# Output projection and feed-forward as one stage in blocks of 512 tokens, with the residual kept on the chip

## The chip, the cores and the metric

The kernel runs on one core of a Trainium2 chip. The metric is the device time of one execution in microseconds (us); lower is better.

## What is computed

One layer of a hybrid decoder (2048 tokens, model width 1024, FFN width 2816). Three token mixers run in parallel and write their outputs into one matrix of 1024 rows of tokens; the change begins behind them. In the words of the reference:

```python
mix = jnp.concatenate([out_a, out_b, out_c], axis=-1) @ w_out
x = x + gate1 * mix

h = rms_norm(x, norm2_gain) * (1.0 + scale2) + shift2
gt, up = jnp.split(h @ ffn_w_gate_up, 2, axis=-1)
x = x + gate2 * ((jax.nn.silu(gt) * up) @ ffn_w_down)

def rms_norm(x, gain):
    xf = x.astype(jnp.float32)
    y = xf * lax.rsqrt(jnp.mean(xf * xf, axis=-1, keepdims=True) + EPS)
    return (y * gain.astype(jnp.float32)).astype(x.dtype)
```

## The kernel before

Everything is stored transposed: features over the 128 partitions (KD = 8 tiles of 128 for the model width, KF = 22 for the FFN width), tokens along the free axis. Five stages follow one another, each in a block of its own with a barrier over all engines at its end: the input projection with the recurrent mixer (`project_in_and_recur`), the operands of the forgetting attention, that attention, the gated linear attention, the output projection (`project_out`) and the feed-forward (`feed_forward`). Within a stage each engine runs its own list of instructions in order, and waits on semaphores; nothing but these lists and waits sets the order. A stage can't load anything before the barrier ahead of it has opened.

Every product of two float32 matrices is made of three float32r matmuls (`split_products`, L77 to L79): each operand is split into a high part (a copy into float32r) and a low part (the value less its high part). For weights, ScalarE makes the high part and GpSimd the low part, for activations ScalarE and VectorE. One matmul takes a 128x128 tile of weights against 512 tokens.

`project_out` (L1308) loads the eight 128x2048 tiles of `mix_dram` through two buffers (`po_slot`), splits them (L1376 ScalarE, L1404 VectorE), and runs over eight output tiles m; each is 8 x 4 x 3 = 96 matmuls into four banks of 512 tokens. VectorE multiplies by gate1 and adds the residual x (L1409). ScalarE stores the result in HBM (`x_dram`, L1386 and L1391) and squares it (L1388, L1393), GpSimd sums the squares. After the last tile, TensorE takes the mean over the features with a matrix of 1/1024 (L1433, L1436), and ScalarE the root (L1396).

`feed_forward` (L1439) runs over four blocks t of 512 tokens. ScalarE loads the block of x2 back from HBM (L1515, 2 MB); VectorE inverts the root (L1593), scales (L1598), and together with ScalarE makes the split normalised input h (L1511, L1605, L1608). Then come 22 units of gate and up (48 matmuls each; their weights come in one transfer of 1 MB, L1482) and 16 units of down (33 matmuls, 704 KB, L1486; two units for each output tile). Weights have two buffers at every step. The next block's h is made in the down units of the block before. VectorE forms silu(g) * u (L1622) and its low part (L1624), and the output y = x2 + gate2 * d (L1634), for which ScalarE loads x2 from HBM once more (L1535) and stores y (L1539).

The first stage, `project_in_and_recur`, is not touched. It holds 96 units of 24 matmuls (8 x 3) whose weights go through the chain L153 (SP, 512 KB), L239 (ScalarE, high part), L201 (GpSimd, low part) with RAW, HI, LO = 2, 3, 2 buffers, and its instructions are written out, not looped. Its x comes in the same queue, 2 MB for each block (L179).

These lines give the waits of a weight unit there:

```python
                def weights(j):
                    if j >= RAW:
                        sp.wait_ge(lo_ready, j - RAW + 1)
                    sp.dma_start(w_raw[:, j % RAW], w_in[j % N_PROJ]).then_inc(w_sem[j % RAW], 16)
                def low(j):
                    pool.wait_ge(hi_ready, j + 1)
                    if j >= LO:
                        pool.wait_ge(unit_done, j - LO + 1)
```

## Time and profile before

| what | value |
|---|---|
| runs of the kernel before | 3228.06, 3219.3, 3227.46 us (median 3227.46) |
| the profiled execution | 3219.62 us, of which the span of instructions is 3217.8 us |
| TensorE busy in the span | 2821.8 us (88%), mean granted clock 0.926 |
| output projection, first DMA issue to its last product | 1529.85 to about 1726.6 us |
| from there to the first product of the feed-forward | to 1767.27 us |
| feed-forward, first to last product | 1767.27 to about 3214.25 us |

The profile shows one execution; times are from the start of its span. A matmul's printed duration contains the pipeline behind it, so the pitch from one matmul's start to the next is what a matmul costs in a row of many. In a list of waits, the engine named behind the arrow is the one that came last.

### The profile page before, as it was taken

Reading aid. Unit: us, or ns where it says so; the run is one execution under the profiler, and the core shown is the slowest. Engines: PE = TensorE matmul, PEld = TensorE weight load, DVE = VectorE, ACT = ScalarE, POOL = GpSimd, SP = SyncE. Lnnn points to the kernel's source line nnn. Section 1 sums busy time; section 2 is a strip of 40 time slices with the busy share of each in tenths; the row PEclk is TensorE's granted clock in tenths of the full one; section 3 lists DMA queues with packets and bytes.
Section 4 is the critical chain, followed back from the end, with each engine's and each line's share of the span. In section 5 each row is a group of like instructions: output and inputs, shape, how many; then the busy total and the mean of one; then the engine's idle time right before and its main releaser. Section 6 shows DMA issues by size and latency. Waiting matters only on the chain. (4 is left out here: it accounts for less than half of the span.)

```text
span 3217.8 us, 34182 instructions
## 1 busy us (share of the span) xinstructions
PE 2821.8 (88%) x12359; PEld 2250.3 (70%) x12359; DVE 1547.8 (48%) x1627; ACT 1090.5 (34%) x1400; POOL 1088.3 (34%) x420
## 2 busy tenths in 40 slices
PE   3898999945887879556795999999999999999999
PEld 2686878821666667334584888878888788888887
DVE  6878786434565656545214454224440444224420
ACT  2333342341475757443212333222221222222221
POOL 2444454401121212100232343444444443444443
PEclk9999999975798989656898999999999999999999
DMA  5555534436211110200523222442234322432233
GB/s 212 193 173 171 172 125 134 138 131 187 52 47 47 46 47 7 115 0 25 220 108 128 100 92 91 126 147 95 100 98 131 136 91 92 122 125 104 91 98 104
DMA packets 86971, 355.99 MB, mean 111 GB/s; under 512 B 9622, under 2 KB 11430, under 8 KB 64690
## 3 DMA queue, kind: packets, MB, share of 16 engines
q1 hardware_dynamic: 67760, 312.81, 29.1%
q10 hardware_dynamic: 19024, 41.95, 4.3%
q8 instruction: 41, 0.67, 0.1%
q14 instruction: 50, 0.41, 0.0%
q0 software_dynamic: 96, 0.15, 0.0%
HBM read 298.15 MB, written 56.72 MB: 110 GB/s over the span
## 5 line engine op out<-in xcount | busy, mean ns | idle before, releaser
L1492 POOL TENSOR_TENSOR ff_w_lo<-ff_w_raw,ff_w_hi 128x2048 fp32r<-128x2048 f32 (+1 forms) x152 | 613.6, 4037 | 875.9 <-ACT ff_w_hi L1521 875.9
L1624 DVE TENSOR_TENSOR ff_a_lo<-ff_gated,ff_a_hi 128x512 f32 x88 | 382.2, 4343 | 148.4 <-ACT ff_a_hi L1531 148.4
L1521 ACT ACTIVATE ff_w_hi<-ff_w_raw 128x2048 fp32r<-128x2048 f32 (+1 forms) x152 | 256.2, 1686 | 356.0 <-PE ff_d_ps L79 356.0
L201 POOL TENSOR_TENSOR w_lo<-w_raw,w_hi 128x1024 fp32r<-128x1024 f32 x96 | 239.2, 2493 | 286.4 <-PE g_ps L79 220.7
L77 PE MATMUL g_ps<-h_hi,w_hi 128*128 128x512 f32 x768 | 309.4, 403 | 8.5 <-POOL w_lo L201 4.8
L77 PE MATMUL ff_g_ps<-ff_h_hi,ff_w_hi 128*128 128x512 f32 x704 | 275.7, 392 | 37.8 <-DVE ff_h_lo L1608 31.9
L78 PE MATMUL g_ps<-h_lo,w_hi 128*128 128x512 f32 x768 | 301.1, 392 | 0.0
L79 PE MATMUL g_ps<-h_hi,w_lo 128*128 128x512 f32 x768 | 301.1, 392 | 0.0
L79 PE MATMUL ff_g_ps<-ff_h_hi,ff_w_lo 128*128 128x512 f32 x704 | 275.5, 391 | 0.0
L78 PE MATMUL ff_g_ps<-ff_h_lo,ff_w_hi 128*128 128x512 f32 x704 | 275.5, 391 | 0.0
L77 PE MATMUL ff_u_ps<-ff_h_hi,ff_w_hi 128*128 128x512 f32 x704 | 273.9, 389 | 0.0
L78 PE MATMUL ff_u_ps<-ff_h_lo,ff_w_hi 128*128 128x512 f32 x704 | 273.9, 389 | 0.0
L77 PE MATMUL ff_d_ps<-ff_a_hi,ff_w_hi 128*128 128x512 f32 x704 | 273.9, 389 | 0.0
L78 PE MATMUL ff_d_ps<-ff_a_lo,ff_w_hi 128*128 128x512 f32 x704 | 273.9, 389 | 0.0
L79 PE MATMUL ff_d_ps<-ff_a_hi,ff_w_lo 128*128 128x512 f32 x704 | 273.9, 389 | 0.0
L79 PE MATMUL ff_u_ps<-ff_h_hi,ff_w_lo 128*128 128x512 f32 x704 | 273.9, 389 | 0.0
L1527 ACT ACTIVATE ff_silu<-ff_g_ps 128x512 f32<-128x512 f32 x88 | 52.7, 599 | 600.9 <-PE ff_u_ps L79 600.8
L810 POOL TENSOR_TENSOR fa_p_lo<-fa_probs,fa_p_hi 128x512 fp32r<-128x512 f32 (+3 forms) x78 | 93.2, 1195 | 403.4 <-ACT fa_p_hi L847 403.4
L239 ACT ACTIVATE w_hi<-w_raw 128x1024 fp32r<-128x1024 f32 x96 | 101.8, 1060 | 368.4 <-DMA w_raw<-in_w_in 297.4
L874 DVE TENSOR_REDUCE fa_ch_max<-fa_s_ps 128x1 f32<-128x512 f32 (+2 forms) x262 | 158.8, 607 | 138.4 <-PE fa_s_ps L930 77.2
L1622 DVE TENSOR_TENSOR ff_gated<-ff_silu,ff_u_ps 128x512 f32<-128x512 f32 x88 | 60.4, 687 | 341.0 <-ACT ff_silu L1527 341.0
L1634 DVE SCALAR_TENSOR_TENSOR ff_gated<-ff_d_ps,mod,ff_x_res 128x512 f32<-128x512 f32 x32 | 24.0, 751 | 401.9 <-PE ff_d_ps L79 401.9
(249 smaller groups left out, 5455.5 us busy)
## 6 DMA issues: line engine op xcount, KB each, us to landing
ff_w_raw<-in_w_gate_up SPq DMA_DIRECT2D x88, 1024.0 KB, 4.8
w_raw<-in_w_in SPq DMA_DIRECT2D x96, 512.0 KB, 4.0
ff_w_raw<-in_w_down SPq DMA_DIRECT2D x64, 704.0 KB, 4.1
mod_w<-in_w_mod SPq DMA_DIRECT2D x24, 1024.0 KB, 5.5
proj_dram<-stage SPq DMA_DIRECT2D x72, 256.0 KB, 3.2
po_slot<-mix_dram SPq DMA_DIRECT2D x8, 1024.0 KB, 4.9
po_slot<-in_xT SPq DMA_DIRECT2D x8, 1024.0 KB, 4.8
x_dram<-po_slot ACTq DMA_DIRECT2D x8, 1024.0 KB, 3.9
```

Of the source, the lines that this page charges most:

```text
L77: nc.tensor.matmul(out, hi, act_hi, start=first, stop=False)
L78: nc.tensor.matmul(out, hi, act_lo, start=False, stop=False)
L79: return nc.tensor.matmul(out, lo, act_hi, start=False, stop=last)
L201: nc.gpsimd.tensor_tensor(w_lo[:, j % LO], w_raw[:, j % RAW], w_hi[:, j % HI].bitcast(F32), ALU.subtract).then_inc(lo_ready, 1)
L239: nc.scalar.activation(w_hi[:, j % HI], w_raw[:, j % RAW], ACT.Copy).then_inc(hi_ready, 1)
L810: nc.gpsimd.tensor_tensor(p_lo[:, m % PB, r * P:BLK], probs[:, m % PB, r * P:BLK], p_hi[:, m % PB, r * P:BLK].bitcast(F32), ALU.subtract). ...
L874: nc.vector.tensor_reduce(ch_max[:, u % 2, i, c:c + 1], s_ps[:, n % SB, 0:w], AX.X, ALU.max).then_inc(max_done, 1)
L1492: nc.gpsimd.tensor_tensor(w_lo[:, s, size(up)], w_raw[:, s, size(up)], w_hi[:, s, size(up)].bitcast(F32), ALU.subtract).then_inc(lo_ready, 1)
L1521: nc.scalar.activation(w_hi[:, s, size(up)], w_raw[:, s, size(up)], ACT.Copy).then_inc(hi_ready, 1)
L1527: nc.scalar.activation(silu[:, s], g_ps[:, s], ACT.Silu).then_inc(silu_ready, 1)
L1622: nc.vector.tensor_tensor(gated[:, s], silu[:, s], u_ps[:, s], ALU.mult).then_inc(gated_ready, 1)
L1624: nc.vector.tensor_tensor(a_lo[:, bass.ds(n, 1)].rearrange("p o n -> p (o n)"), gated[:, s], a_hi[:, bass.ds(n, 1)].rearrange("p o n -> p ...
```

## The change

`project_out` and `feed_forward` become one stage, `out_and_feed_forward`, with one list of 272 units, each with one load of weights: 8 units "o" (an output tile of the output projection for 512 tokens, 24 matmuls), then for each block 22 pairs "g", "u" (24 matmuls each), four output tiles of down ("d", two units of 33 matmuls each), the eight "o" units of the next block, and the other four output tiles of down. The weights of a gate and up pair come as two transfers of 512 KB. Those of the output projection are loaded and split four times, once for each block. The weight chain has the buffers and waits of the first stage (RAW, HI, LO = 2, 3, 2). x2 stays in SBUF, in two blocks of 512 tokens (`ff_x2`), so that the stores to `x_dram` and the loads from it are gone; x is loaded into it by SP (2 MB for a block, `residual`). The squares are summed by VectorE on 512 tokens; the mean (`mean`) is one matmul for each block. For block 0 it stands behind the eighth "o" unit with the whole norm after it; for later blocks it stands behind the ninth half-tile of down, and the norm is made during the rest. The mixers' outputs for block 0 come in eight transfers of 256 KB, each with a semaphore of its own; the constant for the mean is the last of the first loads, and TensorE waits for it at the mean. The stage's instructions are written out, not looped. All loads and stores are issued by SP.

```diff
...
-def feed_forward(nc, vec, mod, rms_all, w_gate_up, w_down, x2, yT):
...
+def out_and_feed_forward(nc, vec, mod, xT, w_out, w_gate_up, w_down, consts, mix, yT):
...
+    W_MAX = HALF * P
+    units = [("o", 0, m, 0) for m in range(KD)]
+    for b in range(NBLK):
+        for n in range(KF):
+            units += [("g", b, n, 0), ("u", b, n, 0)]
+        units += [("d", b, m, s) for m in range(HALF_KD) for s in range(2)]
+        if b + 1 < NBLK:
+            units += [("o", b + 1, m, 0) for m in range(KD)]
+        units += [("d", b, m, s) for m in range(HALF_KD, KD) for s in range(2)]
+    at = {u: j for j, u in enumerate(units)}
+    N = len(units)
+    width = lambda u: HALF * P if u[0] == "d" else KD * P
+    d_order = {u[:3]: i for i, u in enumerate([u for u in units if u[0] == "o" or (u[0] == "d" and u[3] == 1)])}
+    HI, LO, RAW, DB = 3, 2, 2, 3
...
-        w_hi, w_lo = sb("ff_w_hi", [P, 2, 2 * KD * P], F32R), sb("ff_w_lo", [P, 2, 2 * KD * P], F32R)
+        x2 = sb("ff_x2", [P, 2, KD, BLK])
+        w_raw = sb("ff_w_raw", [P, RAW, W_MAX])
+        w_hi, w_lo = sb("ff_w_hi", [P, HI, W_MAX], F32R), sb("ff_w_lo", [P, LO, W_MAX], F32R)
...
+        g_ps, u_ps, d_ps, n_ps = ps("ff_g_ps", [P, 2, BLK]), ps("ff_u_ps", [P, 2, BLK]), ps("ff_d_ps", [P, DB, BLK]), ps("ff_n_ps", [P, BLK])
...
+                def weights(j):
+                    kind, b, i, s = units[j]
+                    if j >= RAW:
+                        sp.wait_ge(lo_ready, j - RAW + 1)
+                    src = {"o": lambda: w_out[i], "g": lambda: w_gate_up[i, :, 0:KD * P], "u": lambda: w_gate_up[i, :, KD * P:], "d": lambda: w_down[2 * i + s]}[kind]()
+                    sp.dma_start(w_raw[:, j % RAW, 0:width(units[j])], src).then_inc(w_in[j % RAW], 16)
...
+                weights(0)
+                for k in range(KD):
+                    sp.dma_start(x2[:, 1, k], mix[k, :, cols(0)]).then_inc(mix0_in[k], 16)
+                    if k == 1:
+                        weights(1)
+                residual(0)
+                sp.dma_start(mean_ones[:], consts[:, C_MEAN * P:(C_MEAN + 1) * P]).then_inc(const_in, 16)
+                for j in range(N):
+                    kind, b, i, s = units[j]
+                    if j + RAW < N:
+                        weights(j + RAW)
+                    if kind == "g" and i == 2 and b + 1 < NBLK:
+                        residual(b + 1)
+                    if kind == "d" and b + 1 < NBLK and i < HALF_KD:
+                        k = 2 * i + s
+                        if k < 2:
+                            sp.wait_ge(gated_ready, KF * (b + 1))
+                        else:
+                            sp.wait_ge(mix_ready, KD * (b + 1) + k - 1)
+                        sp.dma_start(silu[:, k % 2], mix[k, :, cols(b + 1)]).then_inc(mix_in[k % 2], 16)
...
+                def high(j):
+                    wide = slice(0, width(units[j]))
+                    act.wait_ge(w_in[j % RAW], 16 * (j // RAW + 1))
+                    if j >= HI:
+                        act.wait_ge(unit_done, j - HI + 1)
+                    nc.scalar.activation(w_hi[:, j % HI, wide], w_raw[:, j % RAW, wide], ACT.Copy).then_inc(hi_ready, 1)
+                def mix_high(b, k):
+                    act.wait_ge(*landed(b, k))
+                    if b >= 1:
+                        act.wait_ge(unit_done, at["u", b - 1, KF - 1, 0] + 1)
+                    nc.scalar.activation(h_hi[:, k], staged(b, k), ACT.Copy).then_inc(mix_hi, 1)
...
+                high(0)
+                for k in range(2):
+                    mix_high(0, k)
+                high(1)
+                for k in range(2, KD):
+                    mix_high(0, k)
+                for j in range(N + 1):
+                    if j + 2 < N:
+                        high(j + 2)
+                    if j == 0:
+                        continue
...
+                    if kind == "o" and b == 0 and i == KD - 1:
+                        root(0)
+                        for k in range(KD):
+                            norm_high(0, k)
+                    if kind == "d" and b + 1 < NBLK and i >= HALF_KD:
+                        q = 2 * (i - HALF_KD) + s
+                        if q == 0:
+                            root(b + 1)
+                        for k in pairs_at(q):
+                            norm_high(b + 1, k)
...
+                def scale(b, k):
+                    if k >= 2:
+                        dve.wait_ge(h_ready, KD * b + k - 1)
+                    nc.vector.scalar_tensor_tensor(out=silu[:, k % 2], in0=x2[:, b % 2, k], scalar=scale_a[:, k:k + 1], in1=rstd[:],
+                                                   op0=ALU.mult, op1=ALU.mult).then_inc(xs_ready, 1)
+                def norm_low(b, k):
+                    dve.wait_ge(h_hi_ready, KD * b + k + 1)
+                    nc.vector.scalar_tensor_tensor(out=h_lo[:, k], in0=silu[:, k % 2], scalar=mod[:, SHIFT2 + k:SHIFT2 + k + 1], in1=h_hi[:, k].bitcast(F32),
+                                                   op0=ALU.add, op1=ALU.subtract).then_inc(h_ready, 1)
...
+                        if b == 0 and i == KD - 1:
+                            invert(0)
+                            scale(0, 0)
+                            for k in range(KD):
+                                if k + 1 < KD:
+                                    scale(0, k + 1)
+                                norm_low(0, k)
...
+                def mean(b):
+                    pe.wait_ge(const_in, 16)
+                    pe.wait_ge(summed, (KD - 1) * (b + 1))
+                    if b >= 1:
+                        pe.wait_ge(rms_ready, b)
+                    nc.tensor.matmul(n_ps[:], mean_ones[:], sq_sum[:], start=True, stop=True).then_inc(mean_done, 1)
...
+                        for k in range(KD):
+                            if i == 0:
+                                pe.wait_ge(mix_ready, KD * b + k + 1)
+                            last = split_products(nc, d_ps[:, d % DB], tiles(w_hi, hi, k), tiles(w_lo, lo, k), h_hi[:, k], h_lo[:, k], k == 0, k == KD - 1)
```

The order of three places, as the compiler has it. In these rows the tensor `ff_x2` reads `ff_x`.

SP at the start of the output projection, before: the constant, then mixers of 1 MB alternating with weights, then six mixers that wait, x and more weights.

```order
L1332 DMA po_mean_ones<-in_consts 128x128
L1336 DMA po_slot<-mix_dram 128x2048
L1338 DMA po_w_raw<-in_w_out 128x1024
L1336 DMA po_slot<-mix_dram 128x2048 [waits po_mix_lo] x6
L1341 DMA po_slot<-in_xT 128x2048 [waits po_mix_lo]
```

The same place now: two transfers of weights and eight of the mixers, then x (2 MB) and the constant ahead of the third load of weights.

```order
L1368 DMA ff_w_raw<-in_w_out 128x1024
L1379 DMA ff_x<-mix_dram 128x512 x2
L1368 DMA ff_w_raw<-in_w_out 128x1024
L1379 DMA ff_x<-mix_dram 128x512 x6
L1375 DMA ff_x<-in_xT 128x8x512
L1383 DMA ff_mean_ones<-in_consts 128x128
L1368 DMA ff_w_raw<-in_w_out 128x1024 [waits ff_lo_ready] x6
```

What moved: the first weights went ahead of the mixers, and x ahead of the weights of the third unit.

TensorE between the output projection and the feed-forward, before: two mean products for each of four banks, the end of the stage, the barrier.

```order
L1433 MATMUL po_banks<-rms_all,po_mean_ones 128x512 [waits po_x2_ready,po_added]
L1433 MATMUL po_banks<-rms_all,po_mean_ones 128x512 x3
L1436 MATMUL po_banks<-po_squares,po_mean_ones 128x512 [waits po_squared]
L1436 MATMUL po_banks<-po_squares,po_mean_ones 128x512 x3
L1329 UNCONDITIONAL_BRANCH
L1637 UNCONDITIONAL_BRANCH [waits barrier_Pool_Activation_PE_DVE_SP_release]
L1644 UNCONDITIONAL_BRANCH [waits ff_h_ready]
```

TensorE now, at the mean of block 1, in the middle of the down units of block 0:

```order
L77 MATMUL ff_d_ps<-ff_a_hi,ff_w_hi 128x512
L78 MATMUL ff_d_ps<-ff_a_lo,ff_w_hi 128x512
L79 MATMUL ff_d_ps<-ff_a_hi,ff_w_lo 128x512
L1573 MATMUL ff_n_ps<-ff_sq_sum,ff_mean_ones 128x512 [waits ff_rms_ready,ff_summed,ff_const_in]
L77 MATMUL ff_d_ps<-ff_a_hi,ff_w_hi 128x512 [waits ff_a_ready,ff_lo_ready]
```

What moved: one mean product for each block stands between down units, with no barrier behind it.

VectorE, from the last output tile to the normalised input of block 0, before: the reciprocal, two operations of 2048 columns for half a block each, and the rest in halves, all behind the barrier and the load of x2.

```order
L1586 SCALAR_TENSOR_TENSOR ff_scale_a<-mod,vec 128x8
L1593 RECIPROCAL rms_all<-rms_all 128x512 [waits ff_scaled]
L1598 TENSOR_TENSOR ff_x_blk<-ff_x_blk,rms_all 128x2048 [waits ff_x_in,ff_scaled]
L1605 TENSOR_SCALAR ff_x_blk<-ff_x_blk,ff_scale_a,mod 128x512 [waits ff_h_hi_ready]
L1605 TENSOR_SCALAR ff_x_blk<-ff_x_blk,ff_scale_a,mod 128x512 x3
L1608 TENSOR_TENSOR ff_h_lo<-ff_x_blk,ff_h_hi 128x2048 [waits ff_h_full]
```

VectorE now:

```order
L1532 SCALAR_TENSOR_TENSOR ff_x<-ff_d_ps,mod,ff_x 128x512 [waits ff_x_in,ff_unit_done]
L1538 TENSOR_TENSOR ff_sq_sum<-ff_sq_sum,ff_sq 128x512 [waits ff_summed,ff_squared]
L1499 RECIPROCAL ff_rstd<-ff_rstd 128x512 [waits ff_rms_ready]
L1505 SCALAR_TENSOR_TENSOR ff_silu<-ff_x,ff_scale_a,ff_rstd 128x512 [waits ff_rstd_ready]
L1505 SCALAR_TENSOR_TENSOR ff_silu<-ff_x,ff_scale_a,ff_rstd 128x512
L1510 SCALAR_TENSOR_TENSOR ff_h_lo<-ff_silu,mod,ff_h_hi 128x512 [waits lru_out_stored_2]
```

What moved: the norm of block 0 follows its eighth output tile directly, in two operations of 512 columns for each of eight tiles, and TensorE may take each tile as it comes. (`lru_out_stored_2` is the semaphore that now serves as `ff_h_hi_ready`.)

## Rows read from the trace of the kernel before

**Rows 1.** TensorE's waits from 1529 us on: us in total, times, longest.

```profile
PE ff_g_ps L77 <- DVE ff_h_lo L1608: 31.9, 1, 31.9
PE po_banks L77 <- POOL po_w_lo L1359: 20.6, 1, 20.6
PE ff_g_ps L77 <- DVE ff_a_lo L1624: 5.9, 2, 2.9
```

**Rows 2.** Timeline, start of the output projection: start, us, engine, operation, idle before.

```profile
1529.85 0.34 SPq L1332 DMA_DIRECT2D po_mean_ones<-in_consts  x1
...
1538.42 3.45 POOL L1359 TENSOR_TENSOR po_w_lo<-po_w_raw,po_w_hi 128x1024 fp32r<-128x1024 f32 x1 [6.61 <-ACT po_w_hi L1379]
...
1541.92 0.79 PE L77 MATMUL po_banks<-po_m_hi,po_w_hi 128*128 128x512 f32 x1 [20.56 <-POOL po_w_lo L1359]
```

**Rows 3.** Timeline of TensorE at the end of the output projection.

```profile
1723.64 0.39 PE L79 MATMUL po_banks<-po_m_hi,po_w_lo 128*128 128x512 f32 x1
...
1726.36 0.39 PE L79 MATMUL po_banks<-po_m_hi,po_w_lo 128*128 128x512 f32 x1
1726.59 3.59 PE L1433 MATMUL po_banks<-rms_all,po_mean_ones 128*128 128x512 f32 x8
1731.64 3.70 PE L1436 MATMUL po_banks<-po_squares,po_mean_ones 128*128 128x512 f32 x8 [1.46 <-ACT po_squares L1393]
```

**Rows 4.** Chain that ended last, feed-forward: start, length, what (matmuls: the pitch).

```profile
1736.46 8.22 DMA ff_x_blk<-x_dram
...
1767.27 0.79 PE ff_g_ps L77
1768.06 0.43 PE ff_g_ps L78
...
1772.94 0.23 PE ff_g_ps L78
...
2153.75 0.50 PE ff_g_ps L77
...
3214.41 0.75 DVE ff_gated L1634
```

**Rows 5.** Groups by line and form: busy, mean ns of one, idle before.

```profile
L201 POOL TENSOR_TENSOR w_lo<-w_raw,w_hi 128x1024 fp32r<-128x1024 f32 x96 | 239.2, 2493 | 286.4 <-PE g_ps L79 220.7 <-ACT w_hi L239 65.7
L239 ACT ACTIVATE w_hi<-w_raw 128x1024 fp32r<-128x1024 f32 x96 | 101.8, 1060 | 368.4 <-DMA w_raw<-in_w_in 297.4 <-PE g_ps L79 60.6 <-DVE lru_r_gate L426 10.4
L1492 POOL TENSOR_TENSOR ff_w_lo<-ff_w_raw,ff_w_hi 128x1408 fp32r<-128x1408 f32 x64 | 208.2, 3254 | 288.0 <-ACT ff_w_hi L1521 288.0
L1521 ACT ACTIVATE ff_w_hi<-ff_w_raw 128x1408 fp32r<-128x1408 f32 x64 | 88.4, 1381 | 321.0 <-PE ff_d_ps L79 321.0
L1622 DVE TENSOR_TENSOR ff_gated<-ff_silu,ff_u_ps 128x512 f32<-128x512 f32 x88 | 60.4, 687 | 341.0 <-ACT ff_silu L1527 341.0
L1624 DVE TENSOR_TENSOR ff_a_lo<-ff_gated,ff_a_hi 128x512 f32 x88 | 382.2, 4343 | 148.4 <-ACT ff_a_hi L1531 148.4
L1531 ACT ACTIVATE ff_a_hi<-ff_gated 128x512 f32 x80 | 49.6, 621 | 19.5 <-DVE ff_gated L1622 19.5
L1593 DVE RECIPROCAL rms_all<-rms_all 128x512 f32<-128x512 f32 x4 | 13.4, 3351 | 21.9 <-DMA out_yT<-ff_gated 21.9
L1396 ACT ACTIVATE rms_all<-po_banks,po_eps 128x512 f32<-128x512 f32 x4 | 2.7, 687 | 0.4 <-PE po_banks L1436 0.3
```

**Rows 6.** DMA issues: size of one, median us to landing.

```profile
w_raw<-in_w_in SPq DMA_DIRECT2D x96, 512.0 KB, 4.0
ff_w_raw<-in_w_down SPq DMA_DIRECT2D x64, 704.0 KB, 4.1
x_blk<-in_xT SPq DMA_DIRECT2D x3, 2048.0 KB, 8.6
```

**Rows 7.** Timeline of the first stage, its first unit of 24 matmuls.

```profile
60.63 0.77 PE L77 MATMUL g_ps<-h_hi,w_hi 128*128 128x512 f32 x1 [2.95 <-DVE h_lo L365]
...
70.37 0.69 DVE L384 COPY lru_xa<-g_ps 128x512 f32<-128x512 f32 x1 [1.06 <-PE g_ps L79]
```

**Rows 8.** TensorE's waits in the first stage, 0 to 645 us.

```profile
PE g_ps L77 <- POOL w_lo L201: 4.8, 3, 2.2
```

443 lines of the change are left out of this document (148 added, 295 removed).

## The prediction

> **What bounds the kernel now.** First the waits of TensorE from 1529 us on, since it is busy in 88% of the span and the change touches only this part. In [rows 1] two waits stand out, one in front of the output projection (20.6 us) and one between it and the feed-forward (31.9 us); two of up to 2.9 us stand at the start of blocks of the feed-forward. Everything else runs at the pitch of the products: from 1723.64 to 1726.36 lie 12 pitches [rows 3], 0.2267 us each. The code gives the number of products: 8 x 96 = 768 in the output projection and 4 x (22 x 48 + 16 x 33) = 6336 in the feed-forward, so 174.1 and 1436.2 us. What remains of the two stages is overhead, read from starts in the timeline and in the chain:
>
> - first DMA issue to first product, 1529.85 to 1541.92 [rows 2]: 12.1 us;
> - the output projection itself, 1541.92 to 1726.59 [rows 2, 3]: 184.7 us less 174.1, 10.6 us (slow clock at first, and mixers of 1 MB that come slower than they are used);
> - from the last product to the first of the feed-forward, 1726.59 to 1767.27 [rows 3, 4]: 40.7 us;
> - the feed-forward, 1767.27 to the last operation of VectorE at 3214.41 [rows 4]: 1447.1 less 1436.2, 10.9 us.
>
> The sum is 74.3 us. TensorE is the bound elsewhere in both stages, so the change can give at most this. It doesn't change the number of products (each output tile of 512 tokens is still 24), and it leaves the first four stages alone.
>
> **The change part by part, against the profiled execution.**
>
> *Start.* The first weights (512 KB) are now the first issue. A load of this size lands 4.0 us after its issue [rows 6], the high part takes 1.06 and the low part 2.49 us [rows 5]: 1529.85 + 4.0 + 1.06 + 2.49 = 1537.4. The low part of the first mixer (0.69 us, as an operation of this size in [rows 5]) comes on top, since it must wait for GpSimd or hold it up: 1538.2, and 1538.4 with a little of the 3.45 us that GpSimd's first low part took in [rows 2]. The bounds are 1537.4 (no collision) and 1541.9 (nothing gained). Overhead 8.6 us. That row also shows the collision: VectorE was then making the low part of the first mixer, and GpSimd's operation took 3.45 us where the mean is 2.49. The Trainium skill, SBUF — State Buffer, section "Who interferes with whom", says that an operation of VectorE with two inputs in SBUF and one of GpSimd exclude each other, the second waiting to the end of the first; without that rule the start would be 0.7 us earlier, no more. The constant (64 KB) is waited for 45 us later: nothing.
>
> *First unit.* After a pause the pitch is 0.43 us where it is 0.23 later [rows 4]; from 1767.27 to 1772.7 some 13 products ran so. I take the same here: 13 x 0.2 = 2.6 us. The eight mixers (2 MB) are behind the first weights in the queue. From 4.0 us for 512 KB and 8.6 us for 2 MB [rows 6], 1.5 MB cost 4.6 us, 3.1 us per MB. The eighth mixer is at 3 MB in the queue and lands at 1529.85 + 4.0 + 2.5 x 3.1 = 1541.6, while TensorE reaches it after 21 products, at 1538.4 + 13 x 0.43 + 8 x 0.23 = 1545.8: hidden. The third weights lie at 5.56 MB, behind x, and land by 1549.5; with 1.06 and 2.49 they are ready at 1553.1, when TensorE is through unit 2 at 1538.4 + 8.0 + 5.4 = 1551.8. So 0 to 3 us; since all loads ahead of a load are in flight together, I take 0.
>
> *Norm of block 0.* Let E be the end of the eighth "o" unit. In the list of ScalarE its square stands behind the high part of the third weights ahead. Their load is issued when the low part two units earlier ends (E - 5.4 + 2.5), lands 4.0 later (E + 1.1), the high part ends at E + 2.2, the square 0.62 later and the sum 0.69 later [rows 5]: E + 3.5. In the kernel before, the last mean products began 4.9 us after the end (1726.75 to 1731.64, [rows 3]), with operations four times as wide; that is the upper bound. The mean product takes 3.70 / 4 = 0.9 us for one bank's share [rows 3], twice that at the slow clock: E + 5.0. Root 0.69 and reciprocal 3.35 [rows 5]: E + 9.0. From the reciprocal to the first product are two operations of VectorE and one of ScalarE of 0.62 to 0.7, and the gaps: 2.5. First product at E + 11.5. Its unit is paced by VectorE, two operations for each of eight tiles; the first unit of the first stage had the same work and took 60.63 to 70.37, 9.7 us [rows 7]. End of the unit at E + 21.2 where 5.4 would do: overhead 15.8 us, bounds 13 and 19. This takes the place of 40.7 us and of the slow start of the feed-forward. What is gone is the barrier, the load of x2 (8.22 us, [rows 4]), and three quarters of the width.
>
> *Later blocks.* Their output units stand between down units. The mean product costs 0.9 us each, three times: 2.7. What else is late there must hide under down units of 33 x 0.2267 = 7.48 us. The last part of a after the last up unit: SP issues the third down load 2.2 us before that unit ends, landing 4.1 later [rows 6], high part 1.38, then a's high part 0.62 and low part 0.69: 4.6 us after the unit's end, of 7.48. The sum of squares for the mean by the same steps: 4.6 of 7.48. The eighth mixer's low part behind GpSimd: 3.1 us after the last down unit of the first half, of 7 x 0.68 = 4.8 that TensorE needs to reach it; this is the thinnest cover, 1.7 us, and the cost is the excess if it is gone. The norm has four more down units: hidden. So the waits of 5.9 us in [rows 1] and the slow clock behind them go.
>
> *The weight chain.* Each unit has a load of its own now, and loads of the output projection rise from 8 to 32, all behind two raw buffers. Over two units (10.88 us) the chain takes issue 0.4 + landing 4.0 + 1.06 + 2.49 = 7.95 us; for down 0.4 + 4.1 + 1.38 + 3.25 [rows 5, 6] = 9.1 of 14.96. The first stage has this very chain, with 2 MB of x in the same queue three times; TensorE waited for a low part of weights three times there, 4.8 us in all [rows 8]. Taken as 0 to 4.8 here, I put 2, nearer to nothing, because the first stage also had other loads in that queue. The stores of y and the mixers' loads move to SP; each waits for an event of two units back and lets the next weights pass first. The two loads and stores of x2 (three passes of 8 MB) were hidden except at the norm.
>
> *The sum.* Overhead after: 8.6 + 2.6 + 15.8 + 2.7 + 2 = 31.7 us; before: 74.3. Gain 42.6 us. The profiled execution took 3219.62 us (span 3217.8); it becomes 3177.0. The runs shown are 3219.3, 3227.46 and 3228.06: with the profiled one, two values some 8 us apart, whose cause the trace of one can't show. From their median it would be 3184.9. I take the middle, 3181.
>
> **The rivals.**
>
> *Waits return at the seams* (0.15). The covers in the later blocks are thin and all in-order lists meet there: if one is missed at each of three seams, TensorE waits some 3 us (the 2.9 of [rows 1]) and then runs some 9 products at 0.43 instead of 0.23 (from 2153.75 on, [rows 4]), 1.8 us. That is 14 us: 3195. Against it stand the margins of 1.7 and 2.9 us.
>
> *The front does not start earlier* (0.09), so that this part doesn't do what it says: the mixers' and weights' low parts delay each other to 1541.9 (3.5 us), and the third weights come 3 us late behind x, with a slow clock behind that (2.6). 9 us: 3190.
>
> *The chain is too slow: slower than before* (0.05). If a load of 512 KB lands later than 10.88 - 3.95 = 6.9 us after its issue, the chain sets the pace of the 208 units of 24 products; at 8.0 us a unit takes 5.98 instead of 5.44, 112 us in all: 3293. The gain is used up from 7.3 us on. It would need a load of more than 1 MB ahead of each; [rows 6] and [rows 8] speak against it. The Trainium skill, DMA: Bandwidth & Descriptors, section "Bandwidth", has the rule to batch transfers to 1 MiB or more to reach three quarters of the peak; it speaks against halving the transfers of gate and up. The row of the first stage (4.0 us, hidden in 10.88) says that here a bound on bandwidth is not met, so by the rule the loads would cost more and the time would stay the same.
>
> A remainder of 0.03 lies within 0.3% of before.
>
> **How the numbers follow.** Forecast 3181, 0.68. Its own range: start and norm by their bounds (down to 4 us better, up to 7 worse), the two values of the runs (4 each way): 3172 to 3192. The range of 8 in 10 takes in the front and the seams: 3172 to 3200. 0.3% of this kernel is 9.7 us, about what a measurement can tell from no change. Faster by more: 0.68 + 0.15 + 0.09 = 0.92; within: 0.03; slower: 0.05.
>
> **What would show it.** First product within 8.0 to 9.5 us of the stage's first issue; the third unit without a wait over 1 us; one wait of TensorE of about 11 us in front of the first gate unit and none over 1 us behind it; VectorE's low parts of a (4.34 us on average before, [rows 5]) shorter, without effect on the time. TensorE's busy time stays and the span falls. It would be wrong if TensorE's pitch in a full stretch differed from 0.2267 us, if a wait for a low part of weights returned in every unit, or if written-out instructions came late, which the first stage doesn't show.

## The result, and the profile after

The kernel now takes 3182.28 us (median of four runs, 3177.86 to 3183.16), the kernel before 3226.61 in the same session (four runs, 3219.3 to 3228.06): a ratio of 0.9871, 95% interval 0.9853 to 0.9889. The forecast was 3181, its range 3172 to 3200.

Single executions of one kernel differ by some 8 us, so the traces are compared inside the two stages that the change touches, from the first DMA issue of the stage to the start of VectorE's last operation. Before that is 1529.85 to 3214.41 [rows 2, 4], 1684.56 us; after it is 1533.96 to 3176.44, 1642.48 us. The difference is 42.1 us, where the working gave 42.6. The four stages ahead, which are the same in both (the kernel before has six stages, not five), took 4.1 us longer in the profiled execution of after; that belongs to no part of the change.

TensorE's waits from 1529 us on (us in total, times, longest), which answer to [rows 1]:

```profile
PE ff_d_ps L77 <- DVE ff_h_lo L1495: 17.8, 2, 16.4
PE ff_g_ps L77 <- DVE ff_h_lo L1510: 8.0, 4, 6.6
PE ff_n_ps L1573 <- DVE ff_sq_sum L1538: 3.2, 1, 3.2
```

The wait of 31.9 us between the stages is gone and so are the 5.9 us at the starts of blocks. What is left lies in the first 80 us: a start, a pause of 1.37 us inside the first unit (the second of the two waits in the first row), and the norm of block 0. There is no wait for a low part of weights and none at a seam. The start, in the timeline (start, us, engine, operation, idle before), against [rows 2]:

```profile
1533.96 0.34 SPq L1368 DMA_DIRECT2D ff_w_raw<-in_w_out  x1
...
1535.30 0.43 SPq L1368 DMA_DIRECT2D ff_w_raw<-in_w_out  x1
...
1538.84 2.34 POOL L1414 TENSOR_TENSOR ff_w_lo<-ff_w_raw,ff_w_hi 128x1024 fp32r<-128x1024 f32 x1 [4.78 <-ACT ff_w_hi L1423]
...
1541.88 0.76 PE L77 MATMUL ff_d_ps<-ff_h_hi,ff_w_hi 128*128 128x512 f32 x1 [16.40 <-DVE ff_h_lo L1495]
...
1542.04 1.06 ACT L1423 ACTIVATE ff_w_hi<-ff_w_raw 128x1024 fp32r<-128x1024 f32 x1 [0.67 <-DMA ff_w_raw<-in_w_out]
...
1543.17 2.37 POOL L1414 TENSOR_TENSOR ff_w_lo<-ff_w_raw,ff_w_hi 128x1024 fp32r<-128x1024 f32 x1 [1.99 <-ACT ff_w_hi L1423]
...
1543.65 2.44 DVE L1495 TENSOR_TENSOR ff_h_lo<-ff_x,ff_h_hi 128x512 fp32r<-128x512 f32 x1 [1.31 <-ACT ff_h_hi L1429]
...
1546.15 0.80 PE L77 MATMUL ff_d_ps<-ff_h_hi,ff_w_hi 128*128 128x512 f32 x1 [1.37 <-DVE ff_h_lo L1495]
```

The pause hangs on two engines. VectorE makes the low part of the third mixer from 1543.65 on, while GpSimd, since 1543.17, makes that of the second weights. GpSimd ends at 1545.54 and VectorE 0.55 us after it; alone VectorE needs 0.69 us, would have ended at 1544.34, and TensorE ran out of products only at 1544.78.

And the norm of block 0, with the last operation of VectorE:

```profile
1593.42 0.69 DVE L1538 TENSOR_TENSOR ff_sq_sum<-ff_sq_sum,ff_sq 128x512 f32<-128x512 f32 x1 [1.60 <-ACT ff_sq L1437]
...
1594.26 1.10 PE L1573 MATMUL ff_n_ps<-ff_sq_sum,ff_mean_ones 128*128 128x512 f32 x2 [3.23 <-DVE ff_sq_sum L1538]
...
1596.12 3.35 DVE L1499 RECIPROCAL ff_rstd<-ff_rstd 128x512 f32<-128x512 f32 x1 [2.00 <-ACT ff_rstd L1444]
...
1601.94 0.77 PE L77 MATMUL ff_g_ps<-ff_h_hi,ff_w_hi 128*128 128x512 f32 x1 [6.58 <-DVE ff_h_lo L1510]
...
3176.44 0.75 DVE L1553 SCALAR_TENSOR_TENSOR ff_gated<-ff_d_ps,mod,ff_x 128x512 f32<-128x512 f32 x1 [14.21 <-PE ff_d_ps L79]
```

Groups and DMA issues, against [rows 5] and [rows 6]:

```profile
L1527 DVE TENSOR_TENSOR ff_a_lo<-ff_gated,ff_a_hi 128x512 fp32r<-128x512 f32 x88 | 65.5, 744 | 166.4 <-ACT ff_a_hi L1471 166.4
...
ff_w_raw<-in_w_gate_up SPq DMA_DIRECT2D x176, 512.0 KB, 3.6
```

VectorE's low part of a takes 0.74 us where it took 4.34. GpSimd's operation now has 1024 columns and mostly lies apart from it. TensorE got nothing from this in the middle of a block, where that part was never waited for.

### The profile page after: what moved, and what is told of

Read it like the earlier page. It is cut to its first block, busy times and chain, and to the rows that moved or that the text cites. A ratio compares the mean times of both kernels' runs of the same rounds, so it can differ in the third digit from the quotient of the medians.

```text
span 3179.7 us, 32939 instructions
## 1 busy us (share of the span) xinstructions
PE 2820.6 (89%) x12351; PEld 2251.4 (71%) x12351; DVE 1278.7 (40%) x1719; ACT 1133.8 (36%) x1557; POOL 1125.2 (35%) x524
## 4 chain that ended last, share of the span: by engine, by line
PE 51%; DVE 1%; DMA 0%; ACT 0%; POOL 0%; issue 0%; SPq 0%; ACTq 0%; POOLq 0%
PE ff_d_ps L79 7%; PE ff_d_ps L78 7%; PE ff_d_ps L77 7%; PE ff_u_ps L79 5%; PE ff_u_ps L77 5%; PE ff_u_ps L78 5%; PE ff_g_ps L77 5%; PE ff_g_ps L79 5%; PE ff_g_ps L78 5%; DMA ff_w_raw<-in_w_out 0%; DVE ff_silu L1505 0%; DVE ff_h_lo L1510 0%; PE ff_n_ps L1573 0%; DMA ff_w_raw<-in_w_gate_up 0%; DVE ff_rstd L1499 0%; DVE ff_h_lo L1495 0%
## 5 line engine op out<-in xcount | busy, mean ns | idle before, releaser
L1414 POOL TENSOR_TENSOR ff_w_lo<-ff_w_raw,ff_w_hi 128x1024 fp32r<-128x1024 f32 (+1 forms) x272 | 707.0, 2599 | 923.8 <-PE ff_d_ps L79 361.3
L1423 ACT ACTIVATE ff_w_hi<-ff_w_raw 128x1024 fp32r<-128x1024 f32 (+1 forms) x272 | 309.3, 1137 | 1136.5 <-DMA ff_w_raw<-in_w_gate_up 656.2
L77 PEld LDWEIGHTS g_ps<-h_hi,w_hi 128*128 128x128 f32 x768 | 145.6, 190 | 45.9 <-POOL w_lo L201 7.1
L78 PEld LDWEIGHTS g_ps<-h_lo,w_hi 128*128 128x128 f32 x768 | 145.9, 190 | 32.8 <-issue 3.8
L79 PEld LDWEIGHTS g_ps<-h_hi,w_lo 128*128 128x128 f32 x768 | 145.4, 189 | 31.4
```

The costliest lines, as they stand in the source:

```text
L77: nc.tensor.matmul(out, hi, act_hi, start=first, stop=False)
L78: nc.tensor.matmul(out, hi, act_lo, start=False, stop=False)
L79: return nc.tensor.matmul(out, lo, act_hi, start=False, stop=last)
L1414: nc.gpsimd.tensor_tensor(w_lo[:, j % LO, wide], w_raw[:, j % RAW, wide], w_hi[:, j % HI, wide].bitcast(F32), ALU.subtract).then_inc(lo_re ...
L1423: nc.scalar.activation(w_hi[:, j % HI, wide], w_raw[:, j % RAW, wide], ACT.Copy).then_inc(hi_ready, 1)
```

## The experiments

A stage length below always means the first issue of the stage to the start of VectorE's last operation, in one profiled execution. It leaves out what the four earlier stages did, which took from 1526 to 1537 us in the executions here. Except where it is said, an edit is made to the changed kernel, whose stage length was 1642.5 us, and 1643.2 in a second session.

### x1: the seams opened

The later blocks' output units stand behind all down units of the block before, and the mean and norm directly behind them.

```diff
-        units += [("d", b, m, s) for m in range(HALF_KD) for s in range(2)]
+        units += [("d", b, m, s) for m in range(KD) for s in range(2)]
         if b + 1 < NBLK:
             units += [("o", b + 1, m, 0) for m in range(KD)]
-        units += [("d", b, m, s) for m in range(HALF_KD, KD) for s in range(2)]
...
-                    if kind == "o" and b == 0 and i == KD - 1:
-                        mean(0)
-                    if kind == "d" and b + 1 < NBLK and i == HALF_KD and s == 0:
-                        mean(b + 1)
+                    if kind == "o" and i == KD - 1:
+                        mean(b)
```

> The changed kernel, but the eight output units of blocks 1 to 3 stand behind all sixteen down units, and the mean and the norm of each block directly behind them, as block 0 has it. Nothing is left out. The theory (the norm's chain costs what it costs for block 0 wherever no product stands beside it: 11.0 us of waiting and 5.0 us more in the unit that it paces, by the trace of the change) expects three more waits of 9 to 11 us in front of gate products and 3 x 16 = 48 us in all, about 3230 us, no faster than the kernel before. The rival (the gain came with the barrier and the way over HBM, and the norm in narrow operations is cheap once TensorE is warm) expects under 5 us for each seam, at most 3197 us.

Measured: 3227.88 us, ratio to the kernel before 1.0021 (1.0008 to 1.0034). The stage length is 1690.6 us (1532.02 to 3222.60), 48.1 more than with the seams hidden, so 16.0 for each of three norms in the open. The longest waits of TensorE in it:

```profile
PE ff_g_ps L77 <- DVE ff_h_lo L1503: 31.5, 15, 6.6
PE ff_d_ps L77 <- DVE ff_h_lo L1488: 17.9, 2, 16.7
PE ff_n_ps L1558 <- issue: 9.5, 3, 3.2
```

The theory holds. One stage with x2 in SBUF, but with all four norms in the open, is no faster than the two stages were. The kernel before made the later blocks' h under down units already, so x1 shows what the fusion must keep, and what an open norm costs; it doesn't show that the 42 us came from the order.

### x2: block 0's mixers in one transfer

```diff
-                for k in range(KD):
-                    sp.dma_start(x2[:, 1, k], mix[k, :, cols(0)]).then_inc(mix0_in[k], 16)
-                    if k == 1:
-                        weights(1)
+                sp.dma_start(x2[:, 1], mix[:, :, cols(0)].rearrange("k p n -> p k n")).then_inc(mix0_in[0], 16)
+                weights(1)
```

> Block 0's mixers come in one transfer of 2 MB with one semaphore, in place of eight of 256 KB; all else is the changed kernel's. Theory (the first product waits for the first mixer alone): the first product comes not 7.9 us after the stage's first transfer is issued but after about 12.5 (2 MB landed in 10.4 us where x is loaded, then 0.63 for a high and 1.03 for a low part); the wait of 1.4 us inside the first unit goes, so the stage is 3 to 5 us longer. Rival (the front is set by the first weights, the mixers' sizes are nothing): the first product within 1 us of 7.9.

Measured: 3181.79 us in one run, stage length 1642.4. The start, and the mean of block 0:

```profile
1534.18 0.34 SPq L1368 DMA_DIRECT2D ff_w_raw<-in_w_out  x1
...
1544.89 0.77 PE L77 MATMUL ff_d_ps<-ff_h_hi,ff_w_hi 128*128 128x512 f32 x1 [19.17 <-DVE ff_h_lo L1493]
...
1548.72 0.50 PE L77 MATMUL ff_d_ps<-ff_h_hi,ff_w_hi 128*128 128x512 f32 x1 [0.93 <-DVE ff_h_lo L1493]
...
1594.38 1.10 PE L1571 MATMUL ff_n_ps<-ff_sq_sum,ff_mean_ones 128*128 128x512 f32 x2 [3.20 <-DVE ff_sq_sum L1536]
```

The first product comes 10.7 us after the first issue instead of 7.9, yet the mean begins 60.2 us after it, where it was 60.3. The first product is later, as the theory had it (by less than it said), but the stage is not longer: in the changed kernel the 2.8 us are given back inside the first unit. There it holds a pause of 1.37 us, and the pitch stayed at 0.43 us up to 1551.4, 9.5 us after the first product; here the pause is 0.93 us, and the pitch was 0.23 from 1549.1 on, 4.2 us after the first product. So by these two traces the eight transfers bring nothing. But a part of that is luck of the clock, which comes back at very different times in one and the same kernel (last section). Where it came back early in both, in x10 and in x8's second execution below, the transfers of 2 MB cost 1.1 us of stage length.

### x3: the constant waited for at the head

```diff
+                pe.wait_ge(const_in, 16)
                 for j in range(N):
                     kind, b, i, s = units[j]
```

> TensorE waits for the constant of the mean at the head of the stage instead of at the mean; all else is the changed kernel's. Theory: the constant stands in the queue behind x's 2 MB, issued 5.4 us after the first weights and 10.4 us under way, so the first product comes about 16 us after the first issue instead of 7.9, less the 1.4 us that it then doesn't wait inside its first unit: 6 to 8 us longer. Rival: the constant's 64 KB overtake the 2 MB, and the first product is late by at most 2 us.

Measured: 3190.26 us in one run; the first product comes 18.7 us after the first issue (1533.89 to 1552.54), and the stage length is 1651.1 us, 8.6 more.

```profile
PE ff_d_ps L77 <- DMA ff_mean_ones<-in_consts: 27.1, 1, 27.1
```

The 64 KB don't overtake the 2 MB of x ahead of them in the queue. Waiting for the constant at the mean is therefore worth 8.6 us in this order of transfers; with the constant asked for first, as in the kernel before, it was not tried.

### x4: the kernel before, with its weights not held back

In the kernel before, SP waited for the first block of x2 before it asked for the weights of the feed-forward. This takes the wait away.

```diff
-                sp.wait_ge(x_in, 16)
```

> The kernel before without SP's wait for the block of x2 at the start of the feed-forward, so that the first two transfers of weights leave at once. By the theory that GpSimd and VectorE held each other up there (four operations of VectorE in 10.31 us where the four before took 1.92, beside two low parts of GpSimd in 9.14), GpSimd is through before VectorE comes to the norm, and the 40.7 us between the stages become 32 to 34. The rival (the weights then take bandwidth from the 2 MB of x2, and nothing is won) expects 39 to 42 us, with x2 landing 3 us later.

Measured: 3226.91 us in one run, and both expectations fell. From the mean products to the first product of the feed-forward are 45.6 us (1729.4 to 1775.0) instead of 40.7 [rows 3, 4].

```profile
1739.52 0.41 ACTq L1513 DMA_DIRECT2D ff_x_blk<-x_dram  x1
...
1752.53 4.50 DVE L1596 TENSOR_TENSOR ff_x_blk<-ff_x_blk,rms_all 128x2048 f32<-128x2048 f32 x2 [9.46 <-DMA ff_x_blk<-x_dram]
...
1761.98 10.38 DVE L1603 TENSOR_SCALAR ff_x_blk<-ff_x_blk,ff_scale_a,mod 128x512 f32<-128x512 f32 x4
...
1762.49 9.14 POOL L1490 TENSOR_TENSOR ff_w_lo<-ff_w_raw,ff_w_hi 128x2048 fp32r<-128x2048 f32 x2 [44.81 <-ACT ff_w_hi L1519]
```

With two loads of weights issued beside it, from 1739.92 on, x2's block landed 13.0 us after its issue instead of 8.2 [rows 4]. The weights came earlier and were of no use: their high parts stand behind those of the input in ScalarE's list, so GpSimd began its low parts at the same place in the chain, and the four operations of VectorE beside it took as long (10.38 us) as in the kernel before. There the timeline has the same four operations twice, once without GpSimd and once beside its low parts:

```profile
1750.08 1.91 DVE L1605 TENSOR_SCALAR ff_x_blk<-ff_x_blk,ff_scale_a,mod 128x512 f32<-128x512 f32 x4 [0.80 <-ACT ff_h_hi L1511]
...
1754.23 10.39 DVE L1605 TENSOR_SCALAR ff_x_blk<-ff_x_blk,ff_scale_a,mod 128x512 f32<-128x512 f32 x4
```

So 8.5 of the old 40.7 us are VectorE held beside GpSimd. The prediction's list of what goes there (barrier, load of x2, width) leaves them out. In the changed kernel GpSimd stands still from 1593.5 to 1612.5, while the norm is made, so that they are gone too. x4 was to take them away by themselves and didn't; how the gain at this seam divides between them, the barrier, the load and the width is read from the rows and was not tested.

### x5 and x6: a longer weight chain

Ahead of each load of weights, SP loads a part of the same tile and waits for it: 256 of its columns (128 KB) in x5, 1024 (512 KB) in x6.

```diff
+                    sp.dma_start(w_raw[:, j % RAW, 0:1024], src[:, 0:1024]).then_inc(pre_in, 16)
+                    sp.wait_ge(pre_in, 16 * (j + 1))
                     sp.dma_start(w_raw[:, j % RAW, 0:width(units[j])], src)
```

> As the run that loads everything twice, but the first load is 128 KB. By the theory of two raw buffers the chain is 0.4 + 2.4 + 0.4 + 3.6 + 1.06 + 2.4 = 10.3 us, under 10.88: no wait for weights in full stretches, the time of the changed kernel within 5 us (3177 to 3187). The rival that any longer landing costs in proportion expects about half of what the double load costs, 30 us or more.

> The changed kernel, but SP loads 512 KB of each weight tile, waits for it, and then loads the whole tile again. This doubles the time from the first issue to the weights without a second load in flight. The theory of two raw buffers (the chain issue, landing, high part, low part must fit into two units) expects 0.4 + 3.6 + 0.5 + 3.6 + 1.06 + 2.4 = 11.6 us for two units of 10.88: 0.35 us for each of 208 units of 24 products, 70 us in all (50 to 90), about 3255 us, and waits of TensorE for weights; the down units (13.3 of 14.96 us) don't wait. The rival (a spare factor remains, since loads overlap each other) expects no change within 5 us.

Measured: x5 3201.81 us in one run, stage length 1660.3, 17.8 more; x6 3366.11 us, ratio to the kernel before 1.0454 (1.0433 to 1.0476), stage length 1831.7, 189.2 more. Both cost more than was expected; what they say of the chain itself is clear. First x6, two units of the feed-forward, and the group of low parts of a:

```profile
1794.81 0.33 SPq L1369 DMA_DIRECT2D ff_w_raw<-in_w_gate_up  x1
...
1798.29 2.40 POOL L1417 TENSOR_TENSOR ff_w_lo<-ff_w_raw,ff_w_hi 128x1024 fp32r<-128x1024 f32 x1 [3.50 <-ACT ff_w_hi L1426]
...
1798.77 2.47 DVE L1530 TENSOR_TENSOR ff_a_lo<-ff_gated,ff_a_hi 128x512 fp32r<-128x512 f32 x1 [5.18 <-ACT ff_a_hi L1474]
...
1799.55 0.33 SPq L1371 DMA_DIRECT2D ff_w_raw<-in_w_gate_up  x1
...
1803.52 1.06 ACT L1426 ACTIVATE ff_w_hi<-ff_w_raw 128x1024 fp32r<-128x1024 f32 x1 [4.78 <-DMA ff_w_raw<-in_w_gate_up]
...
1804.65 2.38 POOL L1417 TENSOR_TENSOR ff_w_lo<-ff_w_raw,ff_w_hi 128x1024 fp32r<-128x1024 f32 x1 [3.97 <-ACT ff_w_hi L1426]
...
1807.06 0.33 SPq L1369 DMA_DIRECT2D ff_w_raw<-in_w_gate_up  x1
...
L1530 DVE TENSOR_TENSOR ff_a_lo<-ff_gated,ff_a_hi 128x512 fp32r<-128x512 f32 x88 | 223.2, 2536 | 455.8 <-ACT ff_a_hi L1474 455.8
...
PE ff_d_ps L77 <- DVE ff_a_lo L1530: 21.3, 4, 6.2
PE ff_n_ps L1576 <- issue: 17.2, 3, 6.2
```

From 1794.81 to 1807.06 goes one full turn of the chain, which is shared by two units: 4.74 us for the first load with its wait, 3.97 for the second up to the high part, 1.13 to the low part, 2.41 to its end, when TensorE starts the unit and SP issues again. That is 12.25 us, 6.12 for a unit that needs 5.44. Over the 176 gate and up units the 0.68 us make 120 us. Without the first load the turn would be 7.5 us of 10.88, so the chain sets the pace from a landing of about 7.3 us on (the prediction had 6.9). It also came back at the seams, which I had not counted: TensorE waited four times for the last part of a, 21.3 us in all, and three times, 17.2 us, at the mean. There ScalarE's operation stands in its list behind the high part of down weights that land late (at 1894.34 in the first of these seams), and VectorE's behind it starts beside GpSimd's again, and takes 3.3 us instead of 0.7. The first 90 us cost 20.7 more. These are 179 of 189 us.

In x5 the chain fits, nearly: from 1800 to 3000 us TensorE was busy for 1195.9 us of 1200, against all of it in the changed kernel, 4.1 us lost in some 200 units that are loaded in two steps. More than half of its loss is in the front:

```profile
1536.21 0.34 SPq L1369 DMA_DIRECT2D ff_w_raw<-in_w_out  x1
...
1538.38 0.34 SPq L1371 DMA_DIRECT2D ff_w_raw<-in_w_out  x1
...
1544.16 0.33 SPq L1371 DMA_DIRECT2D ff_w_raw<-in_w_out  x1
...
1552.16 0.79 PE L77 MATMUL ff_d_ps<-ff_h_hi,ff_w_hi 128*128 128x512 f32 x1 [2.82 <-DVE ff_h_lo L1498]
```

The first wait in the queue, from 1536.21 to 1538.38, holds back the mixers, the second to 1544.16 holds back the last six of them, so that the pause in the first unit is 2.8 us and the mean comes 70.5 us after the first issue, 10.2 later than without. Of the other 7.6 us most lie in the steady part, where it is 405.9 us from the second mean to the third instead of 403.5. A blocking wait in SP's queue thus costs most at the place where other transfers stand behind it, and 0.6% in the steady part.

### x7: the second weights later

The idea: the third mixer's high part stands in ScalarE's list behind that of the second weights (1542.04 above), which waited for a load that took 6.7 us to land.

```diff
-                    if k == 1:
+                    if k == 3:
                         weights(1)
...
-                for k in range(2):
+                for k in range(6):
                     mix_high(0, k)
                 high(1)
-                for k in range(2, KD):
+                for k in range(6, KD):
                     mix_high(0, k)
```

> The second weights are asked for behind the fourth mixer tile instead of the second, and their high part stands behind six mixers' high parts on ScalarE instead of two. Theory (the 1.4 us that TensorE waits in its first unit come from the second weights' place): the wait goes, 1 to 1.5 us less. Rival (the wait is the pace of VectorE's low parts beside GpSimd's): it stays above 0.8 us. A third case: the second weights are then late for the second unit, and a wait for them comes up there.

Measured: 3179.17 us, ratio to the kernel before 0.9875 (0.9859 to 0.9892); stage length 1642.5, the same.

```profile
1540.40 0.77 PE L77 MATMUL ff_d_ps<-ff_h_hi,ff_w_hi 128*128 128x512 f32 x1 [16.40 <-DVE ff_h_lo L1495]
...
1544.64 2.37 POOL L1414 TENSOR_TENSOR ff_w_lo<-ff_w_raw,ff_w_hi 128x1024 fp32r<-128x1024 f32 x1 [4.93 <-ACT ff_w_hi L1423]
...
1545.20 2.36 DVE L1495 TENSOR_TENSOR ff_h_lo<-ff_x,ff_h_hi 128x512 fp32r<-128x512 f32 x1 [0.86 <-ACT ff_h_hi L1429]
...
1547.61 0.50 PE L77 MATMUL ff_d_ps<-ff_h_hi,ff_w_hi 128*128 128x512 f32 x1 [1.50 <-DVE ff_h_lo L1495]
...
1555.70 0.50 PE L77 MATMUL ff_d_ps<-ff_h_hi,ff_w_hi 128*128 128x512 f32 x1 [0.97 <-POOL ff_w_lo L1414]
...
1591.83 2.05 PE L1573 MATMUL ff_n_ps<-ff_sq_sum,ff_mean_ones 128*128 128x512 f32 x2 [3.19 <-DVE ff_sq_sum L1538]
...
1600.46 0.77 PE L77 MATMUL ff_g_ps<-ff_h_hi,ff_w_hi 128*128 128x512 f32 x1 [6.59 <-DVE ff_h_lo L1510]
```

The pause didn't go, it moved to the seventh mixer (1.50 us, 7.2 us after the first product). That is the rival's case: again the one low part that VectorE starts beside GpSimd's for the second weights takes 2.36 us instead of 0.69 and ends 0.55 us after it. ScalarE's list only decides which mixer is hit. The third case didn't come up: the second unit's weights were in time. The wait of 0.97 us at 1555.70 is in front of product 49, so it is for the weights of the third unit. They are asked for behind x, and their low part was ready 23.2 us after the stage's first issue. In the changed kernel it was ready after 22.6 and TensorE came to it after 24.3, only 1.7 later. So the third weights bound what any repair of the first unit can give here: x8's second execution and x9 below wait 0.6 and 0.5 us for them.

The pitch rose to full speed 3 us after the first product, and the mean came 59.4 us after the first issue, 0.9 earlier. Then the mean's product (two records) took 2.05 us instead of 1.10, and the first gate product came 8.6 us behind the mean instead of 7.7, so the stage is no shorter.

### x8, x9, x10: block 0's norm under block 1's output projection

The largest term left is the norm of block 0 in the open, some 16 us. It can't stand under down units, because there are none before it. But the tiles of a are unused until the first up unit. So block 1's output units follow block 0's, with block 1's mixers staged in a_hi[:, 8:16] and their halves in a_hi[:, 0:8] and a_lo[:, 0:8], and block 0's norm is made while they run. The norm of block 1 is made under the last down units of block 0, at the same place as now.

```diff
-    units = [("o", 0, m, 0) for m in range(KD)]
+    units = [("o", b, m, 0) for b in range(2) for m in range(KD)]
...
-        if b + 1 < NBLK:
+        if 1 <= b < NBLK - 1:
             units += [("o", b + 1, m, 0) for m in range(KD)]
...
-    staged = lambda b, k: x2[:, 1, k] if b == 0 else silu[:, k % 2]
+    staged = lambda b, k: x2[:, 1, k] if b == 0 else a_hi[:, KD + k].bitcast(F32) if b == 1 else silu[:, k % 2]
+    m_hi, m_lo = lambda b, k: (a_hi if b == 1 else h_hi)[:, k], lambda b, k: (a_lo if b == 1 else h_lo)[:, k]
...
-                    if kind == "o" and b == 0 and i == KD - 1:
+                    if kind == "o" and b == 1 and i == 0:
                         mean(0)
```

> Block 1's output projection is moved directly behind block 0's, with its mixers in the then unused tiles of the activations, and block 0's norm is made under it, as the other blocks' norms are under theirs or under down units. Theory (what is left of the overhead is block 0's norm in the open: 16.1 us over its products from the end of its last unit of output projection to the end of the first gate unit): 14 to 16 us less than the changed kernel, about 3167. Rival (the eight further transfers of 256 KB and x's 2 MB in the first 60 us make weights late, or VectorE, which then evicts, sums and scales in one stretch, becomes late for the first gate unit): waits of TensorE of 5 us or more in that stretch, 3172 or above.

Measured: 3166.40 us, ratio to the kernel before 0.9834 (0.9817 to 0.985). Its stage length is 1627.4 us, 15.1 less than the changed kernel's. This is the theory's case. TensorE's waits in the whole stage are one row, the start and the pause, and from 1600 us on it is busy without a break (100% of each window; one stands here) (the windows' columns are us, then busy time and count of PE, PEld, DVE, ACT, POOL, granted clock, DMA share, GB/s):

```profile
PE ff_d_ps L77 <- DVE ff_h_lo L1506: 17.6, 2, 16.5
...
1600.00:1640.00 40.00, 40.00 (x178) 33.15 (x177) 34.06 (x31) 17.50 (x23) 17.10 (x7) 1.00 0.33 100
```

In 1600 to 1640 VectorE is busy for 34 of 40 us, with evictions, sums and the norm, and still nothing waits for it.

Four kernels were then timed side by side on one chip, with nine runs of the kernel before (3223.72 us). The changed kernel itself:

> The changed kernel itself, for the comparison of the next ones on the same chip: 3176 to 3184.

Measured: 3179.05 us, 0.9861 (0.9843 to 0.988). The new order again:

> Block 1's output projection under which block 0's norm is made, again, beside the changed kernel: 14 to 16 us under it, since its stage was 15.1 us shorter by the trace. Rival (part of the difference was drift of the untouched stages): 10 us or less.

Measured: 3162.06 us, 0.9814 (0.9799 to 0.9829), 17 us less than the changed kernel beside it; stage length 1626.1, 17.1 less. That is a little more than was expected, and the rival (drift) is out. In this execution the first unit was through earlier, and a short wait for the third unit's weights came up behind it:

```profile
PE ff_d_ps L77 <- POOL ff_w_lo L1421: 0.6, 1, 0.6
```

The new order with x7's edit:

> The same with the second weights behind the fourth mixer tile too. With the front alone changed, the mean of block 0 came 0.9 us earlier after the stage's start, and the norm's chain gave it back in the open. Theory (here nothing in the open gives it back): 0.5 to 1.5 us less than without it. Rival: no difference (within 0.5), because slow clock or a wait for the second weights takes its place.

Measured: 3164.19 us, 0.9819 (0.9804 to 0.9834), stage length 1626.1: no difference, the rival's case. (The pause is gone from this trace: its first 14 products ran at the slow pitch, and TensorE came to the held low part later.) And with the mixers of either block in one transfer of 2 MB:

```diff
-                    if 1 <= j <= 4:
-                        for k in (2 * j - 2, 2 * j - 1):
-                            sp.wait_ge(mix0_in[k], 16)
-                            sp.dma_start(a_hi[:, KD + k].bitcast(F32), mix[k, :, cols(1)]).then_inc(mix0_in[k], 16)
+                    if j == 1:
+                        sp.dma_start(a_hi[:, KD:2 * KD].bitcast(F32), mix[:, :, cols(1)].rearrange("k p n -> p k n")).then_inc(mix0_in[1], 16)
```

> The same as with block 0's norm under block 1's output projection, but each of the first two blocks' mixers come in one transfer of 2 MB. With the front alone changed so, the first product came 2.8 us later and the mean of block 0 at the same time. Theory (the first unit's pause and the slow clock take back whatever the earlier first product gains): within 1.5 us of the kernel with sixteen transfers. Rival (block 1's 2 MB make weights late): 3 us or more longer, with waits for low parts of weights in the first eight units.

Measured: 3169.73 us, 0.9836 (0.9821 to 0.9852), which is 7.7 us more; but the stage length is 1627.2 us, 1.1 more, and there is no wait for weights in it. The rest lies in front of the stage: its first issue came at 1537.3 us in this execution and at 1527.5 in x8's second. Whether the later start belongs to this kernel or to the execution that was profiled is open; its five times are 3167.6 to 3176.0 us, those of the order before it 3158.8 to 3168.3.

## Why the prediction was right, point by point

The terms, overhead over 1610.3 us of products, in the same steps:

| step | predicted | measured |
|---|---|---|
| first issue to first product | 8.6 | 7.9 |
| first unit | 2.6 | 5.5 |
| block 0's norm and first gate unit | 15.8 | 15.9 |
| later means | 2.7 | 2.6 |
| weight chain, rest | 2.0 | 0.3 |
| sum | 31.7 | 32.2 |

The kernel before had 12.1, 10.6, 40.7 and 10.9 us for the start, the output projection, the seam and the rest of the feed-forward, so these gave 4.2, 5.1, 24.8 and 8.0. That the sum is met within 0.5 us is partly luck: the first unit cost 2.9 us more than was put down, and the start and the weight chain 2.4 less. Two slips in the working change nothing: 1537.4 and 0.69 make 1538.1, not 1538.2, and 3181 less two times 4 is 3173, not 3172. Of its signs most came: no wait over 1 us at the third unit or behind the first gate product, TensorE busy for 2820.6 us after 2821.8, a pitch of 0.227 us. The first product came just under its 8.0 to 9.5 us, and the one wait of 11 us was two, of 3.2 and 6.6, around the mean.

**Start.** The first product came 7.9 us after the first issue, 0.1 before the stretch named for it. GpSimd's first low part took 2.34 us instead of 3.45 [rows 2], and VectorE's first one, from 1540.28 on, still fell on its end (in x3 the same operation stands alone in its row, with 1.29 us instead of 0.69): the collision that was assumed for this place. x2 and x3 show what the two parts of this term rest on, the first mixer and the constant. But this term and the next hang together: x2 lost 2.8 us here and got them back there.

**First unit: the mis-sized term.** It was put at 2.6 us, 13 products at the slow pitch, and measured 5.5: 1.4 of pause and 18 slow products. The working said that the eighth mixer lands before TensorE reaches it, from the bytes ahead of it in the queue, and looked at the queue alone. The mixers did land in time. What it left out is that the collision which it counted for the first mixer comes again at GpSimd's next operation, for the second weights, and holds the third mixer's low part for 2.44 us instead of 0.69. x7 shows the same pause at another mixer. The 18 slow products, where 13 were taken, are the clock's scatter (last section).

**Norm of block 0.** The mean came 3.4 us after the end of the last unit (3.5 predicted), the first gate product 11.1 after (11.5), the end of its unit, where the first up product starts, 21.4 after (21.2), paced by VectorE: one tile in 1.45 us. Root and reciprocal took 0.69 and 3.35 as in the rows of before. x1 repeats it three times at 16.0 us, and x8 takes it out for 15.1 and 17.1. Its size at this seam was right; that the old gap held 8.5 us of VectorE beside GpSimd was not in the account (x4).

**Later blocks.** No wait at any seam, and 0.86 us for each mean. The two margins, 1.7 and 2.9 us, held. x6 shows that they are real and small: with the weights later and GpSimd's operation on top of VectorE's, the waits for the last part of a and for the sum came back, 4.0 to 6.2 us each, so the rival's price of 3 us for a missed cover was rather low. (The 16 us of x1 are another case, a norm with no cover at all.)

**Weight chain.** Loads of 512 KB landed 3.6 us after their issue (4.0 taken), and TensorE never waited for them: 2 us were taken and 0.3 is left, in which lies also the time from the last product to VectorE's last operation. That hid more than half of the error in the first unit. The threshold at which the chain decides was 6.9 in the working and is 7.3 by x6.

**Front not earlier** (rival): half of it happened. The start was earlier by the full term, but 2.9 us of it were lost in the first unit. The third weights were not late, but only because TensorE was: the working had them 1.3 us late and put nothing for it. They were ready when it had said (22.6 us after the first issue; 23.3 in the working), and TensorE, which had lost 2.9 us in the first unit, came 1.7 us after that. Where the first unit ran faster (x7, x8's second execution, x9), it waited 1.0, 0.6 and 0.5 us for them.

**The level.** By the working from the profiled execution it would have been 3177.0, and 3184.9 from the median; the middle was taken, and the four runs lie from 3177.9 to 3183.2. The stage lengths bear out that such differences come from elsewhere: for one and the same kernel they agree within 1.4 us (1642.5 and 1643.2; 1627.4 and 1626.1) while its first issue came at 1533.6 and at 1527.5 us.

## What to carry to other kernels

When two stages are made one, see first what each norm or other chain has above it: here the same fusion with its norms in the open gave nothing, and each norm moved under other products gave 16 us. What the saved traffic by itself is worth was not tested. After that, look for the one seam that has nothing to stand under and ask which later work could be moved there and which memory is still unused at that time. Where VectorE and GpSimd both make halves, look at which operations start beside each other at a start or a seam; in the full stretches it cost nothing here. And judge a start by the end of its first units, not by its first product: the first product may come 3 us earlier and the units end at the same time, and the third load may bound them all.
